# A decoder step with 32 experts: weight loads in order of use, the pair matrix rebuilt from places, and small jobs moved

## The reference, cut to what matters

```
# router: one of 4 groups, then the top 2 of its 8 experts, for each token
comb = (g_w[:, None, None] * oh_g[:, :, None] * w_e[:, None, :])
for g in range(N_EXPERT_GROUPS):
    h = silu(einsum('nd,edf->nef', xt, w_gate[g])) * einsum('nd,edf->nef', xt, w_up[g])
    y = y + einsum('nef,efd->nd', h * comb[:, g, :, None], w_down[g])
x2 = layer_norm(ALPHA * x1 + y)
x3 = layer_norm(ALPHA * x2 + sigmoid(x2 @ w_ple_gate + b) * (p @ w_ple))
```

## Time and profile before

| what | us |
|---|---|
| median of three runs | 592.07 (590.85 to 595.0) |
| profiled execution, device time | 588.4 |
| its span | 586.7 |
| first expert's first matmul to `moe_done` | 277.01 to 515.53 |

### The profile page before, as it was taken

The page is one execution under the profiler, slowest core; times in us unless marked ns, Lnnn a source line. Parts: engine busy times, 40 slices in busy tenths (PEclk is TensorE's granted clock), DMA queues, the critical chain, the costliest instruction groups (busy, mean ns, idle before and its releaser), DMA issues.

```text
span 586.7 us, 9606 instructions
## 1 busy us (share of the span) xinstructions
PE 535.3 (91%) x3664; PEld 385.7 (66%) x3664; DVE 291.4 (50%) x621; ACT 193.1 (33%) x363; POOL 58.7 (10%) x86
## 2 busy tenths in 40 slices
PE   7899879999999979998999999998888899959992
PEld 7899768888999978766654444544444444446771
DVE  3443786555574865686722222222222222259976
ACT  4434444443462360163241111111111121345433
POOL 2000003322443420000000000000000000000121
PEclk9999999999999989969999999999999999979997
DMA  8996336865323940195739999999999999950001
GB/s 280 368 349 201 110 117 204 261 200 163 133 84 101 323 170 2 58 424 234 280 139 426 420 422 424 420 422 421 423 423 421 422 421 419 366 210 1 1 37 54
DMA packets 47565, 151.88 MB, mean 259 GB/s; under 512 B 3105, under 2 KB 27878, under 8 KB 35105
## 3 DMA queue, kind: packets, MB, share of 16 engines
q1 hardware_dynamic: 42754, 136.93, 60.4%
q0 software_dynamic: 3728, 12.08, 6.6%
q10 hardware_dynamic: 1046, 2.37, 1.2%
HBM read 148.59 MB, written 2.90 MB: 258 GB/s over the span
## 4 chain that ended last, share of the span: by engine, by line
PE 65%; DMA 14%; DVE 11%; ACT 3%; issue 3%; SPq 2%; POOL 1%; DVEq 0%; POOLq 0%; ACTq 0%
PE bank L1813 15%; PE bank L1494 15%; DMA ring<-in_w_up_dram 11%; PE bank L1454 8%; PE bank L1826 7%; PE bank L1682 5%; DMA ring<-in_w_in_dram 3%; PE bank L1835 2%; PE bank L1912 2%; PE bank L1760 2%; PE bank L1549 1%; ACT arena L630 1%; DVE gw_low L1320 1%; PE bank L1819 1%; PE bank L1563 1%
## 5 line engine op out<-in xcount | busy, mean ns | idle before, releaser
L1813 PE MATMUL bank<-ring,arena 128*64 128x256 f32 x1024 | 128.8, 392 | 10.6 <-DMA ring<-in_w_up_dram 7.3
L1813 PEld LDWEIGHTS bank<-ring,arena 128*64 128x64 f32 x1024 | 71.0, 134 | 66.6 <-issue 27.2
L1243 DVE TENSOR_TENSOR arena<-bank,arena 128x512 f32 x32 | 22.1, 692 | 143.7 <-PE bank L1835 143.7
L1494 PE MATMUL bank<-x_high,w_high 128*128 128x320 f32 x248 | 79.0, 319 | 2.1 <-ACT arena L592 2.1
L1494 PE MATMUL bank<-x_low,w_high 128*128 128x320 f32 x248 | 76.7, 309 | 0.0
L1494 PE MATMUL bank<-x_high,w_low 128*128 128x320 f32 x248 | 76.5, 308 | 0.0
L1826 PE MATMUL bank<-ring,arena 128*64 128x512 f32 x256 | 61.9, 604 | 0.0
L895 DVE TENSOR_TENSOR w_low<-ring,w_high 128x1024 fp32r<-128x1024 f32 x32 | 40.1, 1260 | 27.3 <-ACT w_high L574 27.2
L1494 PEld LDWEIGHTS bank<-x_high,w_high 128*128 128x128 f32 x248 | 46.6, 188 | 3.7 <-issue 3.6
L1494 PEld LDWEIGHTS bank<-x_low,w_high 128*128 128x128 f32 x248 | 46.7, 188 | 0.1
L1494 PEld LDWEIGHTS bank<-x_high,w_low 128*128 128x128 f32 x248 | 46.6, 188 | 0.0
(11 more groups left out here) (303 smaller groups left out, 884.0 us busy)
## 6 DMA issues: line engine op xcount, KB each, us to landing
ring<-in_w_gate_dram SPq DMA_DIRECT2D x32, 1024.0 KB, 18.1
ring<-in_w_up_dram SPq DMA_DIRECT2D x32, 1024.0 KB, 20.1
ring<-in_w_down_dram SPq DMA_DIRECT2D x32, 1024.0 KB, 16.8
ring<-in_w_in_dram SPq DMA_DIRECT2D x16, 1024.0 KB, 11.0
arena<-in_cache_k_dram POOLq DMA_DIRECT2D x16, 256.0 KB, 3.7
arena<-in_cache_v_dram POOLq DMA_DIRECT2D x16, 256.0 KB, 3.8
ring<-in_w_o_dram SPq DMA_DIRECT2D x4, 1024.0 KB, 10.7
ring<-in_w_ple_gate_dram SPq DMA_DIRECT2D x4, 1024.0 KB, 15.6
```

The lines of the kernel that those rows point to most:

```text
L1243: V.tensor_tensor(YsT[:, :, bass.ds(place, WIN)].rearrange("p (d c) n -> p c d n", d=2), b[:, :].rearrange("p (c d n) -> p c d n", c=4, d= ...
L1494: last = mm(bank[j % 2][:, 0:T], w[:, j % 4, k, :], x[:, k, :], start=(k == n == 0), stop=(k == KD - 1 and n == 2))
L1813: last = mm(b[WIN * f:WIN * (f + 1), 0:256].rearrange("p (s n) -> p s n", s=2), x[:, WIN * k:WIN * (k + 1)], w[:, :, k, f, :], start=(k == ...
```

## The change

Four things are done together. The loads of the experts are issued in the order in which TensorE uses and frees the slots: gate and up of expert n+1 come ahead of down of expert n, in the first filling, in the loop and at the end, and the waits follow the same order; the twelfth unit of the first filling (down of expert 4) thereby stands behind gate and up of expert 5. `turn_pairs` and `pairs_out` go: `spread_places` instead transposes a broadcast of `pos1` and of `pos2` (three transposes each) into two PSUM banks, so that each partition holds the places of all 320 tokens, and VectorE compares them with a new constant column holding each partition's place number (`pairs(n)`, two instructions for each of the five blocks); this is done in the last group of experts, and the combining products wait for it block by block. In the first group, `down` of expert 2 now follows the second gather half directly, then the product of the slot weights, then `turn_result` of expert 1; ScalarE waits for that before it copies the next result. VectorE makes the places and `permutation(0)` ahead of the third low part, and TensorE's wait on the parts is split by tile. Embedding job 2 moves from ahead of the first gather to between the third and the fourth turn of the loop, which becomes two loops of three turns on TensorE and ScalarE. The table of constants grows by five columns.

```
+    c[:, C_PAIR:C_PAIR + 5] = p + P * np.arange(5)[None, :]
...
-        PAIR_BANKS = (4, 5, 4, 5, 4)
-        EMBED_BANKS = (3, 4, 5, 7, 6)
-        EMBED_FIRST = 3
+        EMBED_BANKS = (3, 4, 6, 7, 6)
+        EMBED_FIRST = 2
...
# SP queue
-            for e in range(4):
-                for r, (w, k) in enumerate(((wg_d, KD), (wu_d, KD), (wd_d, 2))):
-                    load(U_EXPERT + 3 * e + r, w[e], k)
+            def load_pair(e):
+                load(U_EXPERT + 3 * e, wg_d[e], KD)
+                load(U_EXPERT + 3 * e + 1, wu_d[e], KD)
+
+            def load_down(e):
+                load(U_EXPERT + 3 * e + 2, wd_d[e], 2)
+
+            def load_again(slot, w, k, expert):
+                src = w[bass.ds(expert, 1), :, :, :].rearrange("o p k n -> p (o k) n")
+                sp.dma_start(unit(slot, k), src).then_inc(w_in_slot[slot], 16)
+
+            load_pair(0)
+            for e in range(1, 5):
+                load_pair(e)
+                load_down(e - 1)
             with sp.Fori(0, EARLY // 4 - 1) as i:
                 for j in range(4):
-                    for r, (w, k) in enumerate(((wg_d, KD), (wu_d, KD), (wd_d, 2))):
-                        slot = 3 * j + r
-                        sp.wait_ge(main["gu"] if r < 2 else main["y"], i * 4 + (j + 1))
-                        src = w[bass.ds(i * 4 + (j + 4), 1), :, :, :].rearrange("o p k n -> p (o k) n")
-                        sp.dma_start(unit(slot, k), src).then_inc(w_in_slot[slot], 16)
-            for e in range(EARLY, EXPERTS):
-                for r, (w, k) in enumerate(((wg_d, KD), (wu_d, KD), (wd_d, 2))):
-                    load(U_LATE + 3 * (e - EARLY) + r, w[e], k)
+                    sp.wait_ge(main["gu"], i * 4 + (j + 2))
+                    load_again(3 * ((j + 1) % 4), wg_d, KD, i * 4 + (j + 5))
+                    load_again(3 * ((j + 1) % 4) + 1, wu_d, KD, i * 4 + (j + 5))
+                    sp.wait_ge(main["y"], i * 4 + (j + 1))
+                    load_again(3 * j + 2, wd_d, 2, i * 4 + (j + 4))
+            for e in range(EARLY + 1, EXPERTS):
+                load_pair(e)
+                load_down(e - 1)
+            load_down(EXPERTS - 1)
...
# ScalarE
-            def pairs_out():
-
-                for c in range(5):
-                    if c == 2:
-                        for hf in range(2):
-                            act.wait_ge(ct_set, 2 + hf)
-                            nc.scalar.copy(slot_weight[:, 320 * hf:320 * (hf + 1)], bank[6 + hf][:, 0:320]).then_inc(weight_set, 1)
-                    act.wait_ge(ga_ps, 16 + c + 1)
-                    nc.scalar.copy(Pj[:, c, :], bank[PAIR_BANKS[c]][:, 0:T]).then_inc(pj_set, 1)
+            def weights_out():
+
+                for hf in range(2):
+                    act.wait_ge(ct_set, 2 + hf)
+                    nc.scalar.copy(slot_weight[:, 320 * hf:320 * (hf + 1)], bank[6 + hf][:, 0:320]).then_inc(weight_set, 1)
 
             gate_sigmoid(main, 1, bank[0])
             for n in range(1, 4):
...
                 if n == 2:
                     for j in range(KD, 2 * KD):
                         gathered(j)
-                    pairs_out()
+                    weights_out()
+                    act.wait_ge(main["yt"], 1)
                 result_out(main, n)
-            with act.Fori(0, EARLY // 4 - 1) as i:
+            with act.Fori(0, 3) as i:
                 four_experts(i * 4 + 5)
-            for j in range(EMBED_FIRST, 5):
+            embedding_out(2)
+            with act.Fori(3, EARLY // 4 - 1) as i:
+                four_experts(i * 4 + 5)
+            for j in range(3, 5):
                 embedding_out(j)
...
# VectorE
             part_low(1)
-            dve.wait_ge(high_set, TILES)
-            V.tensor_tensor(in_groups(x_part[4][64:P, :]), grouped(x1[0:64, 2, :]), in_groups(x_part[4][0:64, :].bitcast(F32)), ALU.subtract).then_inc(low_set, 1)
 
             dve.wait_ge(rank_ps, 1)
             rank = bank[7][:, 0:96].rearrange("p (t n) -> p t n", t=3)
...
                 V.tensor_copy(PT[64:P, 2, c], PT[0:64, 2, c].bitcast(F32)).then_inc(pt_set, 1)
 
             permutation(0)
+            dve.wait_ge(high_set, TILES)
+            V.tensor_tensor(in_groups(x_part[4][64:P, :]), grouped(x1[0:64, 2, :]), in_groups(x_part[4][0:64, :].bitcast(F32)), ALU.subtract).then_inc(low_set, 1)
 
             dve.wait_ge(rank_ps, 2)
             off = bank[6][:, 128:160]
...
                         slot_weights()
                         dve.wait_ge(starts_set, 1)
                         dve.wait_ge(weight_set, 2)
+                        dve.wait_ge(ga_ps, 2 * KD)
                     if j > 0:
                         before = place(j - 1)
                         put(main, j, bank[4 + (j + 1) % 2], before)
 
-            def four_experts(first, last_pick=4):
+            def pairs(n):
+
+                if n == 0:
+                    dve.wait_ge(rank_ps, 3)
+                number = cst[:, C_PAIR + n:C_PAIR + n + 1]
+                link(V.tensor_scalar(Pj[:, n, :], bank[6][:, 0:T], number, None, ALU.is_equal))
+                V.scalar_tensor_tensor(Pj[:, n, :], bank[7][:, 0:T], number, Pj[:, n, :].bitcast(F32), ALU.is_equal, ALU.add).then_inc(pj_set, 1)
+
+            def four_experts(first, last_pick=4, pairs_too=False):
 
                 for j in range(4):
                     hidden(main, first + j, bank[j % 2])
...
                         pick(j % 2, place(first + (j + 1)), main["xg"])
                     before = place(first + (j - 2))
                     put(main, first + (j - 1), bank[4 + (j + 1) % 2], before)
+                    if pairs_too and j > 0:
+                        pairs(j - 1)
...
-            four_experts(EARLY + 1, 2)
+            four_experts(EARLY + 1, 2, True)
             last_place = place(EXPERTS - 1)
             crowded = dve.value_load(flag[0:1, 0:1], min_val=0, max_val=1)
+            pairs(3)
+            pairs(4)
...
# TensorE
-            embedding(2)
-            pe.wait_ge(high_set, TILES)
-            pe.wait_ge(low_set, TILES)
             def gather(j, parts, t):
 
                 for part in parts:
...
                 gather(j, (4,), 2).then_inc(ga_ps, 1)
 
             for parts, t, permutation in (((0, 2), 0, 1), ((1, 3), 1, 2), ((4,), 2, 4)):
+                pe.wait_ge(high_set, t + 1)
+                pe.wait_ge(low_set, t + 1)
                 pe.wait_ge(pt_set, permutation)
                 for j in range(6):
                     if t == 0 and j == EMBED_BANKS[0]:
...
                         pe.wait_ge(starts_set, 1)
                     gather_all(j)
 
-            def turn_pairs():
+            def spread_weights():
 
                 pe.wait_ge(ga_out, 16)
-                for n in range(5):
-                    if n == 2:
-                        pe.wait_ge(ct_set, 1)
-                        for hf in range(2):
-                            mm(bank[6 + hf][:, 0:320], ones[:, :], CT[:, 320 * hf:320 * (hf + 1)], start=True, stop=True).then_inc(ct_set, 1)
-                    if n >= 2:
-                        pe.wait_ge(pj_set, n - 1)
+                pe.wait_ge(ct_set, 1)
+                for hf in range(2):
+                    mm(bank[6 + hf][:, 0:320], ones[:, :], CT[:, 320 * hf:320 * (hf + 1)], start=True, stop=True).then_inc(ct_set, 1)
+
+            def spread_places():
+
+                pe.wait_ge(pe_out, 6)
+                for b, pos in ((bank[6], pos1), (bank[7], pos2)):
                     for t in range(TILES):
                         r = ROWS[t]
-                        last = nc.tensor.transpose(bank[PAIR_BANKS[n]][:, P * t:P * t + r], PT[0:r, t, P * n:P * (n + 1)].bitcast(F32), ident[0:r, 0:r])
-                    last.then_inc(ga_ps, 1)
+                        last = nc.tensor.transpose(b[:, P * t:P * t + r], pos[0:r, t:t + 1].to_broadcast([r, P]), ident[0:r, 0:r])
+                last.then_inc(rank_ps, 1)
 
             def gate_up(q, slot, x, b, halfway=None):
 
...
 
             def turn_result(q, n, b):
                 if isinstance(n, int) and n == 1:
-                    pe.wait_ge(pj_set, 5)
+                    pe.wait_ge(ga_out, 16)
                 pe.wait_ge(q["ys"], n)
                 for c in range(4):
                     last = nc.tensor.transpose(b[:, P * c:P * (c + 1)], y_s[:, P * c:P * (c + 1)], ident)
                 last.then_inc(q["yt"], 1)
 
-            def four_experts(first, slots, here, behind=(2, 2, 2, 2)):
+            def four_experts(first, slots, here, behind=(2, 2, 2, 2), places_too=False):
 
 
                 for j in range(4):
...
                     here(j, 1)
                     gate_up(main, slots[3 * j], xg[:, j % 2, :], bank[j % 2],
                             (lambda: turn_hidden(main, first + (j - 1))) if behind[j] > 0 else None)
+                    if places_too and j == 0:
+                        spread_places()
                     if behind[j] == 3:
                         other_half()
```

(25 more changed lines are left out.)

## The result

The changed kernel took 582.2 us as the median of four runs (579.73 to 582.75), the kernel before 591.46 beside it (587.75 to 595.0): the ratio on record, which is not simply that of the two medians, is 0.9852, with an interval of 0.9807 to 0.9897. A second time, beside the experiments, it was 581.93 against 591.19, 0.9860 (0.9822 to 0.9897). It is faster by about 1.4%: 8 to 9 us by the ratios, 9.3 us by either pair of medians. Two runs in which the clock granted to TensorE averaged 0.74 and 0.65 where all others had 0.96 to 0.98, one of the kernel before (671.09 us) and one of an experiment (755.88 us), are left out of every median and ratio here. The two profiled executions differ less, 588.4 and 582.34 (spans 586.7 and 580.7), because the profile of before was one of the short executions of its kernel.

What follows compares the result with a forecast made beforehand. Transfers and TensorE alternate as limits; when transfers run without a hole sets the expert phase's end. Expert 32 moves from 502.08 to 491.6, gaining 10.5 us: 592.07 - 10.5 = 581.6 us, range 579.0 to 587.5.

Steps and rivals of the forecast that it cites:

- Head: Up to expert 1: third low part and embedding job 2 moved, gather near 267.7, expert 1 1.63 us earlier.
- Experts 3 to 4: Stretch from the end of `gate_up` 3 to `gate_up` 4, claimed to shrink from 13.58 to 9.67 us.
- Loads: SP's load queue: gate and up no longer behind an older `down`, so the transfer hole shrinks to 1.1 us.
- Embeddings and places: Later experts: job 2's 1.28 us hidden in 5.2 us of slack; six new transposes cost 1.0 us.
- Pairs: VectorE's tail: three pair blocks, 2.8 us ahead of `put` 32, hidden by TensorE's idle time, cost taken as 0.
- Pairs on the path: Rival at the tail: TensorE's 3.5 us begin at `moe_done`, so all 2.8 us are added, 584.4; chance 0.15.
- Hole: Rival in the load stream: the hole stays, 585.4 with only the head's gain, 591.4 at old length; chance 0.14.
- Slower loop: Rival at TensorE's split loop: four jumps back at 5.71 us each raise the time by 17.6 to 599.2; chance 0.05.

Runs made afterwards that it cites:

- the four blocks: The changed kernel with four more pair blocks on VectorE's tail, writing blocks 3 and 4 again: 585.44 us, ratio 0.9933 to the kernel before.

## Why the prediction was right, point by point

The time, 581.6, and the mechanism hold: the hole in the loads was the cost, it shrank from 11.4 us to 2.5, and the tail hid the pairs. Of these 8.9 us 7.3 reached expert 28. At expert 32, behind the six new transposes, 6.2 are left (7.3 in the second profile), where 10.5 were said. That the median still met the forecast so closely is in part luck. The 10.5 us were worked out on a profiled execution of 588.4 us and taken off a median of 592.07. From profile to profile only 6.1 us came (588.4 to 582.34), and 577.9 was the sum for that execution; the medians fell by 9.3, because the runs of the kernel before lie about 3 us above its profile and those of the kernel after do not (582.2). What makes the runs of the kernel before longer is not known, and beside the other experiments its medians were 588.5 and 588.9. In ratios the gain is 8 to 9 us, about two less than the 10.5 promised.

- **Head: right in place, wrong in length.** The gather started at 268.00 (267.7 said; `part_low(1)` was itself 0.4 later, at 264.13 instead of 263.73). Then it took 7.69 us at a clock that had been taken for granted, and expert 1 started at 276.79, not 275.4. 1.63 was counted for the head and 0.22 came, an error of 1.4 us.
- **Experts 3 to 4: right.** From 290.36 to 300.00 are 9.64 us, 9.67 were said. ScalarE's new wait was costed at nothing, by a margin of 0.3 us for the chain of `put` 1 and `hidden` 3 on VectorE; there was none, and TensorE waited 0.45 in the middle of `gate_up` 4 ("a few tenths" was the other bound). It was VectorE's chain that came late, by its register read, as the run with the early read shows.
- **Loads: right, with a shorter reach.** "Order of use by itself gives nothing" holds for the count of units, and the run with the order alone shows that not standing behind an older `down`, which is part of the order, is worth 5.6 us by itself. The issue for expert 8 came at 304.96, 2.16 us after the 302.8 said: 1.4 of the head, 0.45 of the stall, 0.3 besides. From there to expert 28 it took 160.0 us, not 158.0, the far end of the 158.1 to 160.0 of like kernels. These two, 4.1 us together, are all that is missing at expert 28 (460.8 said).
- **Embeddings and places: right.** Expert 28 to 32 is 30.92 us, 29.85 before: 1.07 for the six transposes, 1.0 said. Job 2 was costed at 1.28 us, a third of the 12-record row; that row holds only jobs 3 and 4, with 4 and 8 records, and job 2's own row had 1.98. In the loop it took 1.98 (385.00 us), hidden as said, in a slack of 4.5 us by that figure and not 5.2.
- **Pairs: right in effect.** A block is 1.05 us, not 0.93: the one-operand instruction takes 0.55 us, 0.379 on its nearest row. The Trainium skill, "VectorE: DVE Perf Modes", section "Why PSUM operands drop a tier", had said that a float32 instruction loses its double read with a PSUM operand; the trace agrees, 0.55 against 0.38 us for the same instruction with its source in SBUF. The cover held, 0.8 us was left of it, and two runs show that it is the branch. `moe_done` came 3.4 us earlier, not 8, and the first turn 6.1, not 10: both lack what is missing at expert 32.
- **Rivals.** Pairs on the path: refuted, TensorE's idle time is the branch's and not a wake-up's; it decides from 0.8 us more work on, as the four blocks show. Hole: 2.5 us of it stayed, 1.1 said. Slower loop: refuted, experts 8 and 9 stand 6.49 us apart across a turn (326.52 and 333.01), as before. The Trainium skill, "Runtime: NRT & Kernel Launch", section "Instruction fetch mechanics", lets a taken branch stall where its target is not fetched: the trace agrees at the skipped branch, with the packet fetched within the idle time, and shows no such stall at the turns.

## What to carry to other kernels

A queue that stands at a wait for an old buffer holds back all loads behind it: look for the window without bytes, find the wait by the last issue ahead of it, and reorder so that what is free first is asked for first; shortening the stretch that the wait covers works on the same hole (5.6 and 5.7 us here, 9.3 together). Idle time with no releaser at a skipped branch is a cover for other engines' work, and in the trace a wait of its own as soon as they have none (3.4 us here, not shown in the median). Make the sum against a typical execution, not only the profiled one.

## What was not expected of the hardware

TensorE's granted clock fell to 1.2 GHz for 3.4 or 6.8 us around the first gather in all twelve profiles where the embedding job ahead of it was gone, also in the two where products of 512 columns had been put in its place, and cost 1.5 us in the kernel after. A skipped branch of TensorE held it for 5.6 to 6.2 us in ten of twelve profiles and for at most 4.9 in one; at least one packet of instructions, about 16 KB (25 such packets are 0.41 MB on the page of the kernel after), was fetched in that time, where a turn of a loop cost nothing that could be seen. And the three programs with one more copy of a loop body ended 1.0 to 1.1 us later behind their last store, with a fetch of instructions there.
